# Moving the rotary half-swap of eleven projection units from TensorE to transfers, together with a new order of units, retention and attention

## The reference

```python
qa, ka, va, qr, kr, vr, gr = jnp.split(h @ w_in, SPLITS, axis=-1)     # 22 column blocks of 128
qa = rms_norm(heads(qa), q_norm_g)                                    # attention queries
ka = rms_norm(heads(ka), k_norm_g)                                    # attention keys
...
def apply_rope(x, cos, sin):                                          # qa, ka, qr, kr of the latents
    half = HEAD_DIM // 2                                              # HEAD_DIM = 64
    x1, x2 = x[..., :half], x[..., half:]
    return jnp.concatenate([x1 * c - x2 * s, x1 * s + x2 * c], axis=-1)
...
att_x = latent_attention(rope(qa_x), rope(ka_x), va_x, ka_c, va_c)    # softmax over 256 + 512 keys
ret_x = bidir_retention(rope(qr_x), rope(kr_x), vr_x, ..., st_f, st_b)  # chunks of 128, both directions
mix = concat([att_x, head_group_norm(ret_x) * silu(gr)]) @ w_out
```

## Time and profile before

| | |
|---|---|
| time, median of 3 runs | 1646.24 us (1645.33 to 1646.28) |
| the profiled execution: time, span | 1647.73 us, 1646.0 us |
| PE busy | 1506.2 us, 92% of the span |
| DVE, ACT, POOL busy | 59%, 32%, 11% |
| chain of work that ended last | PE 80%, DVE 13% |
| units of `w_in` on PE | from 73.3 us to 266.1 us |
| retention on PE, to the first `scores` | from 266.1 us to 312.2 us |
| attention on PE, to the first unit of `w_out` | from 312.2 us to 446.1 us |

### The profile page before, as it was taken

The page is one execution under the profiler, slowest core; times in us unless marked ns, Lnnn a source line. Parts: engine busy times, 40 slices in busy tenths (PEclk is TensorE's granted clock), DMA queues, the critical chain, the costliest instruction groups (busy, mean ns, idle before and its releaser), DMA issues.

```text
span 1646.0 us, 17024 instructions
## 1 busy us (share of the span) xinstructions
PE 1506.2 (92%) x6206; PEld 1143.7 (69%) x6206; DVE 966.4 (59%) x1216; ACT 518.8 (32%) x728; POOL 178.4 (11%) x137
## 2 busy tenths in 40 slices
PE   7599999899996999999998889996587999999996
PEld 6488777544574888888884258872475888888885
DVE  6834576665517666665215836658944888887222
ACT  1422342333435323222222512330134333333221
POOL 4400040000030000000111400005602000000000
PEclk9999999988998999999997889999698999999998
DMA  7321111132322666665222013220011232223321
GB/s 259 115 96 52 65 65 39 39 102 77 103 77 92 226 214 221 218 219 175 89 91 89 13 64 102 89 77 0 0 64 64 90 102 89 91 100 118 106 70 51
DMA packets 43596, 165.18 MB, mean 100 GB/s; under 512 B 4859, under 2 KB 5435, under 8 KB 42460
## 3 DMA queue, kind: packets, MB, share of 16 engines
q1 hardware_dynamic: 43548, 164.55, 29.4%
HBM read 162.44 MB, written 2.10 MB: 100 GB/s over the span
## 4 chain that ended last, share of the span: by engine, by line
PE 80%; DVE 13%; issue 2%; ACT 2%; POOL 2%; DMA 1%; SPq 0%; POOLq 0%; DVEq 0%; ACTq 0%
PE PS L528 64%; PE PS L783 2%; DVE tb L1539 2%; PE PS L876 2%; PE PS L748 2%; PE PS L747 1%; PE PS L585 1%; DVE H L1539 1%; PE PS L962 1%; PE PS L575 1%; POOL acc L1458 1%; PE PS L770 1%; DVE wsp L517 1%; DVE zpD L2052 1%; DVE RT L1720 1%
## 5 line engine op out<-in xcount | busy, mean ns | idle before, releaser
L528 PE MATMUL PS<-H,wsp 128*128 128x512 f32 x3600 | 840.9, 395 | 27.1 <-DVE H L1539 17.8
L528 PEld LDWEIGHTS PS<-H,wsp 128*128 128x128 f32 x3600 | 681.4, 190 | 181.0 <-issue 21.6
L517 DVE TENSOR_TENSOR wsp<-wraw,wsp 128x1024 fp32r<-128x1024 f32 (+1 forms) x182 | 237.6, 1306 | 468.6 <-ACT wsp L511 468.5
L511 ACT ACTIVATE wsp<-wraw 128x1024 fp32r<-128x1024 f32 (+1 forms) x182 | 202.7, 1115 | 551.9 <-PE PS L528 550.8
L528 PE MATMUL PS<-hid,wsp 128*128 128x512 f32 x1056 | 239.7, 389 | 0.0
L528 PEld LDWEIGHTS PS<-hid,wsp 128*128 128x128 f32 x1056 | 198.2, 188 | 41.2
L1539 DVE SCALAR_TENSOR_TENSOR cva<-PS,dert,cva 128x441 f32<-128x441 f32 (+2 forms) x176 | 122.2, 694 | 5.5
L1455 POOL COPY acc<-sqb 128x512 f32<-128x512 f32 x5 | 5.1, 1012 | 820.9 <-ACT sqb L1278 282.1
L1458 POOL TENSOR_TENSOR acc<-acc,sqb 128x512 f32<-128x512 f32 x35 | 57.5, 1644 | 227.9 <-ACT sqb L1435 93.3
L1748 DVE CUSTOM_DVE_ANT_0 sink<-mring,crow_t,colt 128x1024 bf16<-128x1024 f32 x56 | 71.7, 1280 | 0.4
L1789 DVE TENSOR_REDUCE dert<-PS 128x1 f32<-128x768 f32 x32 | 30.6, 956 | 51.2 <-PE PS L748 51.2
(11 more groups left out here) (275 smaller groups left out, 1458.5 us busy)
## 6 DMA issues: line engine op xcount, KB each, us to landing
mring<-mod_c SPq DMA_DIRECT2D x56, 512.0 KB, 4.5
wraw<-w_ffn_in SPq DMA_DIRECT2D x44, 512.0 KB, 3.3
wraw<-w_up SPq DMA_DIRECT2D x44, 512.0 KB, 3.3
wraw<-w_mod_b SPq DMA_DIRECT2D x24, 512.0 KB, 3.3
wraw<-w_hy_in SPq DMA_DIRECT2D x24, 512.0 KB, 3.2
wraw<-w_w_in SPq DMA_DIRECT2D x22, 512.0 KB, 3.3
wraw<-w_ffn_out SPq DMA_DIRECT2D x16, 704.0 KB, 4.0
wraw<-w_down SPq DMA_DIRECT2D x16, 704.0 KB, 4.0
```

The source lines that it names most:

```text
L511: nc.scalar.activation(wsp[:, o % 2, 0, 0:n], wraw[:, g % RAW, 0:n], ACT.Copy).then_inc(w_hi, 1)
L517: nc.vector.tensor_tensor(wsp[:, o % 2, 1, 0:n], wraw[:, g % RAW, 0:n], wsp[:, o % 2, 0, 0:n].bitcast(F32), ALU.subtract).then_inc(w_lo, 1)
L528: mm = nc.tensor.matmul(psum, wsp[:, o % 2, a, wk * P:(wk + 1) * P], h[:, b, kt, :], start=first and kt == kts[0] and (a, b) == (0, 0), st ...
```

## The change

1. The order of the units: the gates come at n = 10 to 13, the attention queries at 14 to 17 and the retention queries at 18 to 21. Key transposes, decays and states start four units sooner (n = 11 on) and use one PSUM bank for the transposes.
2. `half_swap` on POOL replaces the product with `swap` for eleven of the thirteen roped units (5 to 9 and 14 to 19): four transfers of 32 partitions by 512 columns (64 KB) from `RU` to a tile `RS`, issued by POOL after `q_ev`. DVE waits for them on `q_mv`. Units 20 and 21 keep the product, in banks 4 and 5 by turns. POOL's list of decay matrices (`Dm`) stands between these transfers.
3. The norm's root is `Ln` and `Exp` on ACT in place of a square root on ACT and a reciprocal on DVE.
4. The latent parts of units 0 and 1 both come ahead of their context parts.
5. `aux(21)` and one more turn of DVE's loop are added behind the last unit; `query_decay(0)`, `key_low` and the exponentials `qd` move into the loop.
6. PE's and DVE's orders in retention and attention are rewritten: `inter` before `inner_values`, one `inner` on each side of it; `modulation_row` stands nowhere in retention, never between the last maximum and `shift_low` of an even head, and three rows of it stand behind head 6; `query_low` is taken apart and stands between the maxima.
7. The second half of `crow_t` is loaded and put through Silu later (ahead of `ffn_in`), and some tiles lie elsewhere.

```diff
+        def half_swap(n):
+            pool.wait_ge(q_ev, n + 1)
+            if rope_count(n) >= 2:
+                pool.wait_ge(q_done, rope_count(n) - 1)
+            if n == NQR + 1:
+                pool.wait_ge(r_qd, 2)
+            for block in range(4):
+                to, of = block * HALF, (block ^ 1) * HALF
+                ins = pool.dma_start(moved_tile(n)[to:to + HALF, :], RU[of:of + HALF, n % 2, 0:L])
+                ins.then_inc(q_mv[n % 2], 16)
...
@@ PE, aux(n)
-                    if n > NV:
-                        pe.wait_ge(q_done, n - NV)
-                    nc.tensor.matmul(PS[:, 4, :], swap[:, :], RU[:, n % 2, 0:L], start=True, stop=True).then_inc(q_sw, 1)
+                    if not moved_by_dma(n):
+                        pe.wait_ge(q_rt, 5)
+                        nc.tensor.matmul(PS[:, swap_bank(n), :], swap[:, :], RU[:, n % 2, 0:L], start=True,
+                                         stop=True).then_inc(q_sw, 1)
...
-                if 15 <= n < 21:
-                    key_transposes(n - 15)
-                if n >= 16:
-                    key_states(n - 16)
+                if 11 <= n < 17:
+                    key_transposes(n - 11)
+                if 12 <= n < 18:
+                    key_states(n - 12)
+            aux(21)
...
@@ ACT
-                    SC.activation(RT[:, 0:L], PS[:, 5, :], ACT.Sqrt, bias=col("eps")).then_inc(q_rt, 1)
+                own(SC.activation(RT[:, 0:L], PS[:, 5, :], ACT.Ln, bias=col("eps")))
+                w_ = LA if m == NV else L
+                SC.activation(RT[:, 0:w_], RT[:, 0:w_], ACT.Exp, scale=-0.5).then_inc(q_rt, 1)
...
@@ DVE
-                    dve.wait_ge(q_sw, m - NV + 1)
+                    if moved_by_dma(m):
+                        dve.wait_ge(q_mv[m % 2], 64 * move_count(m))
+                        swapped = moved_tile(m)[:, :]
...
-                        own(VE.reciprocal(RT[:, 0:w_], RT[:, 0:w_]))
...
@@ kernel()
-    order = [va] + [vr + i for i in range(4)] + [ka] + [kr + i for i in range(4)] + [qa + i for i in range(4)] + \
-            [qr + i for i in range(4)] + [gr + i for i in range(4)]
+    order = [va] + [vr + i for i in range(4)] + [ka] + [kr + i for i in range(4)] + [gr + i for i in range(4)] + \
+            [qa + i for i in range(4)] + [qr + i for i in range(4)]
```

More of the change, by code:

```diff
@@ L324, in build, with roped, rope_count, normed_head @@
         NROPE = 13
+        NG = 10
+        NQA = 14
+        NQR = 18
+        def roped(n):
+            return NV <= n < NG or n >= NQA
+        def rope_count(n):
+            return n - NV if n < NG else n - NV - 4
+        def normed_head(n):
+            return n == NV or NQA <= n < NQR
+        def swap_bank(n):
+            return 4 + n % 2
+        def moved_by_dma(n):
+            return roped(n) and n < NQR + 2
+        def moved_tile(n):
+            return RS[n % 2 + (1 if n >= NQR and n % 2 else 0)]
+        def move_count(n):
+            return len([m for m in range(n + 1) if moved_by_dma(m) and m % 2 == n % 2])
         SIDE_TAPS = (3, 5, 0, 1, 2, 6, 7, 8)
@@ L786, in _ @@
             inner(0)
+            inter(0)
             inner(1)
-            for t in range(NPAIR):
+            inner(2)
+            inner_values(0)
+            inner(3)
+            row_max(0, 0)
+            for t in range(1, NPAIR):
+                inter(t)
+                gn_variance(t - 1)
                 if t < 3:
                     inner(2 * t + 2)
+                    inner_values(t)
                     inner(2 * t + 3)
[L792 to L796, removed]
+                    row_max(0, t)
+                else:
+                    row_max(0, t)
+                    inner_values(t)
             shift_row(0)
@@ L1076, in _ @@
                     continue
-                if n < 18 and n - NV >= 2:
-                    act.wait_ge(q_done, n - NV - 1)
+                if n in (NV, NQA):
+                    SC.preload_act_table_set("natural_log_exp_and_others")
+                if roped(n) and n - NV >= 2:
+                    act.wait_ge(q_done, rope_count(n) - 1)
                 if normed_head(n):
@@ L1244, in _ @@
                 high(3, kt, H[:, 0, kt, :], mod_col(3, kt))
+            act.wait_ge(s_crow, 32)
+            SC.activation(crow_t[:, 1, :], crow_t[:, 1, :], ACT.Silu).then_inc(crow_on, 1)
             def ffn_four(i, first, last):
@@ L1500, in _ @@
             ins.then_inc(r_u, 1)
+            half_swap(NQA)
+            half_swap(NQA + 1)
             pool.wait_ge(r_e, 1)
@@ L1503, in _ @@
                              ALU.add).then_inc(r_dm, 1)
+            for n in range(NQA + 2, NQR + 2):
+                half_swap(n)
             sums(2)
@@ L1723, in _ @@
                         VE.tensor_tensor(dst, dst, RT[:, 0:L], ALU.mult).then_inc(q_done, 1)
-                if 15 <= n < 21:
-                    key_decays(n - 15)
-                if n >= 17:
-                    states(n - 16)
-                if n in (18, 19):
-                    key_low(n - 18)
+                if 11 <= n < 17:
+                    key_decays(n - 11)
+                if 13 <= n < 18:
+                    states(n - 12)
+                if n == 20:
+                    query_decay(0)
+                    key_low(0)
+                elif n == 21:
+                    key_low(1)
             def modulation_row(m):
```

258 lines of the change are left out of this document (146 added, 112 removed).

## The result

The changed kernel takes 1598.21 us (median of four, 1597.79 to 1599.68) where the kernel before, run beside it, takes 1645.78 (1644.89 to 1646.28). The ratio is 0.9713, with a 95% interval from 0.9696 to 0.973: 47.6 us less, where 47.0 were predicted. The profiled execution took 1598.33, with a span of 1596.5; before it was 1647.73 and 1646.0, so the two traces lie 49.4 apart, 1.8 more than the medians.

A forecast was written before the change was run, and what follows sets the result against it. PE was taken to bound the kernel, working or waiting for most of the span. The terms 3.0 + 3.6 + 10.6 + 11.4 + 20.4 - 1.0 - 1.0 made 47.0 off 1646.2: 1599 us, range 1590 to 1617.

The forecast's parts named there:

- Units 0 and 1: First units: with unit 1's latent part ahead of the context parts, PE reaches the value transposes sooner, 3.0 us gained.
- The product with `swap`: Units 6 to 9: four products of 0.86 us each leave PE, with 0.2 of a wait, 3.6 us gained.
- Units 10 to 21: From unit 10 to the end of the units: 80.1 us of PE work instead of 90.7, 10.6 us gained.
- The transfers: Half-swaps issued by POOL: four of a unit taken at 6 us, between 2.3 abreast and 9.2 in turn, hidden at 6.
- charge of 1.0 for lateness: Transfers in the units: 1.0 us taken off the gain in case they come late.
- The room of the transfers: Time free before DVE asks for the swapped tile: 6.1 us for a retention query, 6.7 unit 9, 8 or more 5 to 8.
- rival B: Transfers come late: at 10 us for four, 10 lost, 1609; at 14, 25 to 30 lost, 1627; chance 0.20.
- Retention: From unit 21's matmuls to the first scores: 34.7 us instead of 46.1 with the new order, 11.4 us gained.
- Attention: Eight heads: without DVE's work ahead of `shift_low`, stalls and slow clock go, 113.5 us against 133.9, 20.4 us gained.
- Into `w_out`: Start of `w_out`: three modulation rows ahead of DVE's `split_lo` make it end after PE's arrival, 1.0 us lost.

The follow-up runs named there:

- the run with four operations: Changed kernel with four spare POOL operations ahead of each of the eleven units' four transfers: 1603.18 us, ratio 0.9738.
- that with ten: Changed kernel with ten spare POOL operations ahead of each of the eleven units' four transfers: 1630.76 us, ratio 0.9912.
- The two runs with pairs: Changed kernel with the two `inner` of a retention step side by side, once also with `key_low(1)` moved behind `ret_decay(1)` (1598.54 us), once without that (1596.66 us).
- the pairs alone: Changed kernel with the two `inner` of a retention step side by side and `key_low(1)` left between the last two ropes: 1596.66 us, ratio 0.9704.

## Why the prediction was right, point by point

- *Units 0 and 1*: 3.0 predicted, 3.1 in the table, and 3.0 us by its own run. The mechanism and the size held.
- *The product with `swap`*: 0.86 us each held, by the table (3.5 for four units and a wait) and by the run without the transfers (9.5 us for eleven).
- *Units 10 to 21*: 80.1 predicted, 80.6 measured. The products and the root have their own runs. No run has the new order of the units alone, so what it gives by itself is not shown.
- *The transfers*: I took 6 us for a unit's four. By the median they take about 4: the last issue starts 1.5 us behind the first, and a landing takes 2.5. Where DVE waits for them (2.2 us in all), at units 18 and 19, they take 5.9 and 4.7 from the first issue to DVE's going on, so my 6 was not far off there. POOL's and DVE's timelines:

```profile
234.63 1.96 POOL L1565 DMA_DIRECT2D RS<-RU  x4 [5.43 <-ACT RU L1161]
239.79 0.50 POOL L1565 DMA_DIRECT2D RS<-RU  x1 [3.19 <-ACT RU L1161]
241.05 1.49 POOL L1565 DMA_DIRECT2D RS<-RU  x3 [0.76 <-issue]
```

```profile
240.53 0.69 DVE L1815 TENSOR_TENSOR RM<-RU,ropet 128x512 f32<-128x512 f32 x1 [0.25 <-DMA RS<-RU]
...
244.48 0.69 DVE L1815 TENSOR_TENSOR RM<-RU,ropet 128x512 f32<-128x512 f32 x1 [1.93 <-DMA RS<-RU]
...
249.56 0.69 DVE L1815 TENSOR_TENSOR RM<-RU,ropet 128x512 f32<-128x512 f32 x1 [0.88 <-PE PS L667]
```

  The room of 6.1 us that I gave to a retention query wasn't there for unit 19. Its rope follows that of unit 18 without a weight split between them, so DVE asks for the tile 2.8 us behind the first issue (239.79 to 242.55). It comes 1.9 late and costs nothing all the same, since DVE then waits 0.88 for PE's own product of unit 20. So the charge of 1.0 for lateness wasn't needed: PE loses nothing to the transfers, and its 1.26 us ahead of `inner(0)` were in the retention term.
- *The room of the transfers*, in rival B: the point from which lateness costs was placed about right, its price was not. B had 10 us of loss at four microseconds more than the assumed 6. In the run with four operations the first issue of a unit comes 2.7 to 4.0 us later, and it cost 5.0. In that with ten it comes 6.3 to 8.2 later, so with the real 4 some 10 to 12 in all, and it cost 32.6. What failed is the sum of three separate waits: I counted each late rope once. I left out that POOL takes the units in turn, so that DVE was 4 to 6 us late at ten of the eleven ropes, and that each long stop of PE is followed by matmuls at the lower clock. The forecast didn't rest on it, but the upper end of the range did: at a total of 10 to 12 us the kernel is at 1631, where B gave 1609 for 10 and 1627 for 14.
- *Retention*: 11.4 predicted, 9.4 measured; the mechanism held (undoing it costs 9 to 12), the size was 2.0 too high: PE took 36.9 us where I had 34.7. The step of 7.57 us was read where the two `inner` stand together. The change sets them apart, and then they cost 1.09 + 1.08 us and not 1.53 to 1.64, which makes the step 8.0. The second `inter` comes 0.65 later than forecast and the two steps behind it lose 0.9, so 1.5 in all; the rest is small waits at the end. The two runs with pairs confirm it: 7.5 again.
- *Attention*: 20.4 predicted, 21.8 measured. The cause, DVE's own work between the last maximum and `shift_low`, is shown both ways by its two runs. The heads take 14.7 where I took head 2's 15.04 for clean, 2.3 us less over seven of them; head 7 takes 9.0 and not 8.2, by the next point.
- *Into `w_out`*: 1.0 predicted, and it held: DVE's `split_lo` ends at 397.32 and PE starts at 397.46, 2.2 us behind the start of its last matmuls of attention, where it was 1.4 before. The idle time of 0.19 shows only a part of these 0.8 us. Behind it the clock took 1.6 us more, at 0.82, which no term had. It goes with no edit: the same 144 matmuls take 34.6 us in four of the fourteen traces and 33.0 in the other ten, that of the kernel before among them, each time behind the same wait of 1.81 us.

Ahead of `w_out` the terms sum to 48.0 and the traces have 48.7, but retention was 2.0 too high, attention 1.4 too low, and 0.9 came ahead of the first unit; they cancelled. Over the whole program the two traces are 49.4 apart. That the medians come within 0.6 us of the forecast is in part luck; the mechanisms of the large terms are shown by their runs.

## What to carry to other kernels

When a wait of PE is removed, price the stretch behind it too: here three waits with 8.1 us between them were a loss of some 22 to 26, most of it in matmuls at the lower clock. Take the length of a step from a place where its parts stand in the order that they will have, since 16 small matmuls cost 1.64 us in one piece and 2.17 in two. A transfer that takes the place of PE work cost nothing here even where its reader waited 1.9 us, since that reader had to wait for PE soon after. Beyond that slack, and once the queue that issues the transfers is full, the lateness adds up over every such transfer in a row. So measure how far it is, by delaying it, before calling it hidden.

## What the runs showed of the hardware that was not expected

- A transfer of 64 KB within SBUF, issued by GpSimd, keeps its queue for 0.50 us and lands 1.8 to 4.7 us later, 2.5 in the median. The Trainium skill (DMA: Bandwidth & Descriptors, section "Anatomy of one DMA — SWDGE (gpsimd) path") gives about 2.0 us fixed, and an estimate from it made 6 us for four. The trace shows 5.9 and 4.7 for the two units where the end can be seen, and about 4 by the median landing, since issues of 0.50 us overlap with the landings before them.
- The same wait is followed by a lower clock in one execution and not in another. Behind 1.81 us within `w_out` the clock is 0.82 in the changed kernel and 1.00 in the kernel before. Behind 1.26 us ahead of `inner(0)` it is 1.00 in the changed kernel and with the pairs alone, and 0.71 to 0.74 in three other traces. Waits of 2.5 us and more lowered it at each of the twelve places read in the experiments above (0.53 to 0.79 in the windows behind them).
- A DVE operation of 0.68 us took 2.44 once, at 213.49, where POOL's sum over 1024 columns ran from 212.98 to 215.38. Its end, 215.93, lies 0.55 behind POOL's. Before, it was POOL's operation that was stretched.

The timelines of POOL and DVE at that place:

```profile
212.98 2.40 POOL L1585 TENSOR_TENSOR Dm<-Dm,ident 128x1024 f32<-128x1024 f32 x1
```

```profile
213.49 2.44 DVE L1749 TENSOR_TENSOR S<-S,dert 128x512 f32<-128x512 f32 x1
```
